# 160 instead of 128 gathered tokens in layer one's experts; four modulation sums made during the queries; gates in runs of 1 KB

## The reference

```python
def peer(h, w_q, sub_keys, u_tab, v_tab):
    t = h.reshape(b * n, d)                                  # d = 1024
    q = (t @ w_q).reshape(b * n, PEER_HEADS, 2, PEER_KEY_DIM)
    s = jnp.einsum('thcd,hcnd->thcn', q, sub_keys)           # 2 x 128 scores a head
    sv, si = lax.top_k(s, PEER_TOPK)
    cand = (sv[:, :, 0, :, None] + sv[:, :, 1, None, :]).reshape(...)
    score, pos = lax.top_k(cand, PEER_TOPK)
    expert = i1 * PEER_KEYS + i2
    gate = jax.nn.softmax(score, axis=-1)
    act = gelu(einsum('td,thkd->thk', t, u_tab[expert]))
    return einsum('thk,thkd->td', gate * act, v_tab[expert])
```

## Time and profile before

| | us |
|---|---|
| median of 3 runs | 3320.55 |
| lowest, highest | 3320.46, 3329.16 |
| the profiled execution | 3321.39 |
| its span in the trace | 3319.5 |

### The profile page before, as it was taken

The page is one execution under the profiler, slowest core; times in us unless marked ns, Lnnn a source line. Parts: engine busy times, 40 slices in busy tenths (PEclk is TensorE's granted clock), DMA queues, the critical chain, the costliest instruction groups (busy, mean ns, idle before and its releaser), DMA issues.

```text
span 3319.5 us, 52879 instructions
## 1 busy us (share of the span) xinstructions
PE 3176.7 (96%) x20142; PEld 2920.0 (88%) x20142; DVE 2481.6 (75%) x4079; ACT 1466.8 (44%) x1864; POOL 1063.9 (32%) x706
## 2 busy tenths in 40 slices
PE   7999889999999999999999999999988999999999
PEld 5998689856777899999999999998868898989998
DVE  6877568686764479878849999897665797757777
ACT  5434444322443333366633333334234567874443
POOL 0110000010000278877763335551000698721110
PEclk9999899999999999999999999999998999999999
DMA  8984157461012267799999999994203578999996
GB/s 321 333 307 171 47 190 251 160 228 61 4 39 102 94 228 273 267 323 384 380 393 393 379 377 411 409 409 175 93 1 120 183 237 300 386 370 333 351 350 231
DMA packets 305610, 835.27 MB, mean 252 GB/s; under 512 B 22432, under 2 KB 185504, under 8 KB 254368
## 3 DMA queue, kind: packets, MB, share of 16 engines
q1 hardware_dynamic: 180096, 534.82, 44.3%
q0 software_dynamic: 67968, 247.49, 19.3%
q10 hardware_dynamic: 57376, 50.72, 4.5%
HBM read 750.10 MB, written 82.84 MB: 251 GB/s over the span
## 4 chain that ended last, share of the span: by engine, by line
PE 82%; DVE 5%; DMA 5%; ACT 3%; POOL 2%; issue 1%; SPq 1%; another core or an unknown queue 0%; ACTq 0%; DVEq 0%; POOLq 0%
PE ps L3377 16%; PE ps L2936 11%; PE ps L862 7%; PE ps L3360 6%; PE ps L2912 5%; PE ps L1688 5%; PE ps L873 4%; PE ps L3362 3%; PE ps L2310 3%; DMA gates<-arena 3%; PE ps L2914 3%; PE ps L319 3%; PE ps L1430 2%; PE ps L1412 2%; POOL arena_split L2886 2%; PE ps L2150 2%
## 5 line engine op out<-in xcount | busy, mean ns | idle before, releaser
L2886 POOL TENSOR_TENSOR arena_split<-ring,arena_split 128x1024 fp32r<-128x1024 f32 x228 | 570.9, 2515 | 900.6 <-ACT arena_split L2804 898.3
L2936 PE MATMUL ps<-xT_split,arena_split 128*128 128x384 f32 x2048 | 534.0, 337 | 3.1 <-ACT xT L2834 2.6
L3377 PE MATMUL ps<-arena_split 128*128 128x384 f32 x3072 | 532.7, 334 | 2.3 <-DVE arena_split L3300 2.3
L3377 PEld LDWEIGHTS ps<-arena_split 128*128 128x128 f32 x3072 | 532.5, 188 | 2.6 <-issue 2.6
L286 DVE TENSOR_TENSOR arena_split<-ring,arena_split 128x2048 fp32r<-128x2048 f32 x128 | 292.9, 2291 | 245.1 <-ACT arena_split L280 244.3
L3271 ACT ACTIVATE arena_split<-ring 128x2048 fp32r<-128x2048 f32 x126 | 241.7, 1918 | 492.1 <-PE ps L3377 306.6
L280 ACT ACTIVATE arena_split<-ring 128x2048 fp32r<-128x2048 f32 x128 | 244.4, 1915 | 376.9 <-PE ps L862 133.3
L2936 PEld LDWEIGHTS ps<-xT_split,arena_split 128*128 128x128 f32 x2048 | 371.8, 188 | 4.2 <-issue 4.2
L3297 DVE TENSOR_TENSOR arena_split<-ring,arena_split 128x2048 fp32r<-128x2048 f32 x128 | 293.2, 2291 | 94.8 <-ACT arena_split L3271 86.6
L2912 PE MATMUL ps<-hT_split,arena_split 128*128 128x448 f32 x1024 | 338.7, 379 | 6.9 <-POOL arena_split L2886 3.9
L557 POOL DMA_DIRECT2D arena<-in_side_weights x152 | 82.8, 546 | 817.5 <-DVE arena L577 285.0
(11 more groups left out here) (355 smaller groups left out, 6339.9 us busy)
## 6 DMA issues: line engine op xcount, KB each, us to landing
ring<-in_weights SPq DMA_DIRECT2D x396, 1024.0 KB
arena<-in_side_weights POOLq DMA_DIRECT2D x152, 512.0 KB, 5.6
gates<-arena SPq DMA_DIRECT2D x76, 512.0 KB
arena<-gates SPq DMA_DIRECT2D x32, 768.0 KB
arena<-activations SPq DMA_DIRECT2D x64, 384.0 KB
activations<-xT ACTq DMA_DIRECT2D x128, 112.0 KB
arena<-gates SPq DMA_DIRECT2D x32, 448.0 KB
arena<-activations SPq DMA_DIRECT2D x64, 224.0 KB
```

The costliest lines, as they stand in the source:

```text
L2886: pool.tensor_tensor(low, self.raw(f)[:, j, :], high.bitcast(F32), ALU.subtract)\
L2936: mm = pe.matmul(k.ps[:, j, 0:self.T], self.u[:, 2 * (f % 2) + j, a, t * P:(t + 1) * P], self.h[b][:, t, :], start=n == 0, stop=n == 3 * D ...
L3377: mm = pe.matmul(k.ps[:, t, self.from_token:self.from_token + self.T], self.v[:, f % 2, a, j * D + t * P:j * D + (t + 1) * P], self.weight ...
```

## The change

- `GATHERED + SPREAD` = 160 tokens are gathered in layer one, 352 are dense: all dense products have 352 columns, there are 44 lots (pairs 33 to 54), 11 gate blocks.
- The 32 new tokens' 128 slots are spread over the partitions, four groups of 32: 32 more gathers in each half (slots 128 to 159), each with 128 rows of 4 KB. DVE lays out their own vectors (`spread`), TensorE turns them (8 transposes), ACT keeps them in `lru_w`; indices of tile 1 are computed too, and placed by four small copies. The value half has a second total, and `PeerAdd` folds the four groups with a selector matrix.
- Lots take two dots each. Value rows are added at 2.5 a pair, in six buffers in place of five.
- `GATE_ROWS` is 8 in layer one: gates are stored in runs of 8 x 32 x 4 = 1024 bytes, not 512, and loaded every fourth pair.
- Both activation buffers lie in the arena, 352 tokens in one run (one of them was in `xT`, in three runs of 512 bytes).
- The side group `SECOND` keeps parts 0 and 1 (16 tiles, 32 steps). Parts 2 to 5 are a new group `REST` (32 tiles, 32 steps), made during `PeerQuery`, four steps after each chunk's low part, then stored to DRAM (`park`) and loaded again (`reload`) in layer two's `diff_qkv` stage.
- New waits: ACT in `PeerScores` on the first parked sum, ACT in `PeerHidden` on all of them and on the transposes, GpSimd on both before gathering, ACT at value pair 1 on the last stored activations.

```diff
-GATE_ROWS = (4, 4)
+GATE_ROWS = (8, 4)
...
-                       [(1, m, (1, 2) if m < 2 else (1,)) for m in range(6)]]
+                       [(1, m, (1,)) for m in range(2, 6)],
+                       [(1, m, (1, 2)) for m in range(2)]]
...
+    def park(self, pool):
+
+        for i, total in enumerate(self.totals[self.REST]):
+            pool.wait_ge(self.steps.sem, self.steps.at(total[3]))
+            pool.dma_start(self.k.side_dram[:, i, :], self.sums[self.REST][i]).then_inc(self.parked[i > 0].sem, 16)
...
+        if self.side:
+            self.side.begin(dve, self.side.REST)
+            for c in range(8):
+                self.w.low(dve, c, c)
+                self.side.run(self.side.total * (c + 1) // 8)
...
+    def gpsimd(self, pool):
+        if self.side:
+            self.k.enter(pool, self.s)
+            self.side.load(pool, self.side.REST)
+            self.side.park(pool)
+            self.side.wait_parked(pool)
...
-        self.from_token = SPREAD if l else GATHERED
+        self.from_token = SPREAD if l else GATHERED + SPREAD
...
-            self.pair_of += [c] * 3
-        tail = PAIRS - len(self.pair_of)
+            self.pair_of += [c] * (2 * LOTS_PER_PAIR[0])
+        tail = n - len(self.pair_of)
...
+    def place(self, dve, out, rows):
+
+        for g in range(self.groups):
+            ins = dve.tensor_copy(out[g * SPREAD:(g + 1) * SPREAD, :], rows[0:SPREAD, g * SPREAD:(g + 1) * SPREAD])
+        return ins
...
-        self.act = [k.room(8192, 2, 3, P), k.xT[:, 0:6, 0:P].rearrange("p (j x) t -> p j x t", j=2)] if l == 0 else\
+        self.act = [k.room(at, 2, 1, T) for at in (8192, 9600)] if l == 0 else\
...
-                for _ in range(1 + q):
+                for _ in range(2):
                     gather.dot(dve)
...
-        rooms = [15872 + D * i for i in range(3)] + [23552, 24576]
+        rooms = [23552, 24576] + [26624 + D * i for i in range(4)]
...
+            if not self.l and isinstance(c, int) and c == 1:
+                for stored in self.hidden.acts_stored[2:]:
+                    act.wait_ge(stored.sem, stored.at(16 * self.pairs // self.hidden.bufs))
...
-                    self.gather.add(dve, 2 * c)
-            self.gather.add(dve, PAIRS)
+                    self.gather.add(dve, self.gather.rows_total * c // self.pairs)
+            self.gather.add(dve, self.gather.rows_total)
```

199 lines of the change are left out of this document (135 added, 64 removed).

## The result

The changed kernel takes 3349.22 us (median of 6 runs, 3344.83 to 3357.16); the kernel before takes 3323.49 us on the same chip (median of 6, 3318.77 to 3332.17). The ratio is 1.008, 95% interval 1.0066 to 1.0094: 0.8% slower. The forecast was 3308.5 us and faster; the range, 3268 to 3338, does not hold the result.

The account below looks back on a forecast made before the run. It took TensorE and DMA to bound the gates, DMA the tail, and TensorE, DVE and DMA nearly together the value half. The terms 6.5 - 11.5 + 16 - 26 + 3 = -12 us gave 3308.5 us, range 3268 to 3338.

Parts of the forecast that it names:

- step 3: Gate lots and tail of layer one's hidden half: more gathered bytes through DMA cost +16 us (-7 to +36).
- step 2: Hidden half up to the end of routing: shorter products, with DVE not keeping up, give -11.5 us (-19 to -5).
- Step 1: Queries: TensorE waits for a low part placed behind eight side steps, +6.5 us (0 to +9).
- Step 4: Value half of layer one: 507 us in place of 533, -26 us (-41 to -9).
- Step 5: Ends: selecting products, last adds behind TensorE and one more wait for stored activations, +3 us (+1 to +5).
- DMA as it is: After routing and in the value half: DMA moves no faster than before, +24 us in all, 3345 us; chance 0.15.
- The ceiling gives way: Gates, tail and value half: DMA can hold 430 GB/s, -44 us in all, 3277 us; chance 0.25.

Follow-up runs that it names:

- gather_from_6: The changed kernel with the first gather issued at pair 6 of the hidden half in place of pair 8; ratio 1.0059 to the kernel before.
- gate_pieces_early: The changed kernel with two pieces of each gate block stored behind each of two lots, not one behind each of four; ratio 1.0046 to the kernel before.
- at once: The changed kernel with all four pieces of a gate block stored when the block is complete; ratio 1.0044 to the kernel before.
- own_in_psum: The changed kernel with the 32 further tokens' own rows copied back into PSUM before the last 32 dots; ratio 1.0066 to the kernel before.

## Why the prediction was wrong

Two steps failed: step 3, which counted on the buffers to smooth the transfers and so left the stops out of its sum (+40.0 us for +16), and step 2, which priced DVE's operations as if nothing lengthened them (+1.1 for -12.5). Together they are 37.6 of the 44 us by which the sum missed the profiled difference.

- **Step 1, the queries: right in kind, too small.** The wait stood where it was put. The loads took 9.4 us to land against 4 in the row it leaned on the earlier trace rows. +8.6 for +6.5. The 1.4 us on later low parts was said to be hidden.
- **Step 2, to the end of routing: a failed step, 13.6 us.** "From there it works without a gap to 1401" holds in kind: DVE had its first row at 1221.56 and reached its last casts at 1423.2. But that is 201.7 us where before it was 185.4, and the prediction had 4.4 for the added operations. The second index computation with its four copies took 8.4 us for those 4.4 (5.39 of them one conversion), the placing of the weights took 5.0 behind 1423, and the old subtraction 11.7 in place of 2.7: they met GpSimd's low parts. The bound of the step, -5 "if it shares more with a busier GpSimd", names the right engine and is 6 us too small. That DVE had become the limit is confirmed (gather_from_6, 10.5 us); it was in the text, but priced as if its operations kept their lengths.
- **Step 3, gates and tail: the largest miss, 24 us, just outside its own bound.** The price per byte and packet was good: 22 pairs of lots whose stores come at once take 242.4 us in the one profile, predicted 246. (Its share of 1.06 is that of the lots from 1463 us on; the earlier trace rows has the mean with the start, 1.03. Its fast bound uses 137 MB where its own count is 131.8; with that it is 302 us and -20, not -7.) What the sum left out was that the waits come in blocks. The last piece of a gate block has less time to land than it takes at this load; in the long stops it misses by up to 9 us, and TensorE stops. That is 15 us (gate_pieces_early) to 21 us (at once) in the profiles. The rest is the tail, 99.5 us for some 91: the dots from SBUF (own_in_psum gives 6.0 us there), which show as a GpSimd pace of 11.6 us a pair (low parts from 1704.21 to 1773.71, six pairs) for 9.8.
- **Step 4, the value half: right.** 504.5 for 507, DVE 94% busy (473.79 of 503), 401 GB/s at a share of 1.00. The price of a column behind it held too: where nothing waits, 612 products of 352 columns take 159.9 ns each, predicted 160.1.

```profile
2192.17 97.83 PE ps L3489 x612
```

- **Step 5, the ends: +6.7 for +3.** 2.5 us lie between the last value product and layer two's first product (38.0 for 35.6). The other 4 fall into the first 130 us behind that; the granted clock of layer two's first 160 us is 0.96 for 1.00, and a lower clock makes products longer, as behind the stops. What lowered it is open.

Of the rivals, the slower one ("DMA as it is", 3345 us, 0.15) gives nearly the measured time. For the whole that is luck: its value half (-9.5 us) is 18.6 too slow and its routing 13.6 too fast. Its term for gates and tail, +36, is close. Its mechanism there is half right: the engines are not at a fixed 369 GB/s, they move 391 to 423 where nothing stops. "The ceiling gives way" is refuted: the full engines of the lots stayed at 424 GB/s and less in every slice, and the value half ran at 401. The chance given to slower was too low: step 3 itself had TensorE asking for 467 GB/s in a stretch whose lots ran at 369 in the mean, and the forecast counted on the buffers to smooth it.

## What to carry to other kernels

When a stretch is full on DMA, price the bytes, and then look for the buffer whose return has a deadline: how long may the last store take to land, and who stops if it is late? A stop costs its length, the slower products behind it, and the DMA time that lies idle once the queues have run out, and here issuing the stores earlier mended it and moving them to another queue did not. Before giving an operation to VectorE beside a GpSimd that works on SBUF, ask whether one of its operands can stand in PSUM, and whether the wait would only pass to the next operation.

## What the runs showed of the hardware

- VectorE operations with two operands in SBUF, and some conversions and copies within SBUF, wait for GpSimd's low part to end (0.23 becomes 5.39 us), and GpSimd's gathers beside such dots take 1.39 us in the mean, up to 1.99, in place of 0.94. With one operand in PSUM neither happens (1221 and 940 ns), and one-operand searches on SBUF do not wait (at most 295 ns).
- After a stop of 8.8 us TensorE's next 40 products take 7.5 us in place of 5.0, at a mean granted clock of 0.62.
- While TensorE stands, full DMA queues go on at 414 to 417 GB/s; the rate falls to 169 to 262 only 17 to 22 us after a stop of 8 to 9 us began.
- A queue of its own does not bring a store home sooner where all queues share full engines: 19 to 21 us from issue to landing on ACT's queue, 22 to 28 on the sync queue.
- Gates stored and loaded in runs of 512 B in place of 1 KB make the whole some 14 us longer (1.0124 for 1.008), of which the profile shows 6.4 in gates and tail.
